# Routing weights placed by two fp16 products per token in place of three bf16 ones, in a two-layer mixer and expert kernel

## The reference, cut to what matters

```python
def one_block(xb):
    q = (xb @ w_q).reshape(tb, PEER_HEADS, 2, PEER_KEY_DIM)
    sc = jnp.einsum('thpk,hpnk->thpn', q, sub_keys).astype(jnp.float32)
    s1, i1 = lax.top_k(sc[:, :, 0], PEER_TOPK)
    s2, i2 = lax.top_k(sc[:, :, 1], PEER_TOPK)
    ...
    top_s, pos = lax.top_k(cand, PEER_TOPK)
    idx = jnp.take_along_axis(cidx, pos, axis=-1)
    gw = jax.nn.softmax(top_s, axis=-1).astype(xb.dtype)
    act = jax.nn.gelu(jnp.einsum('td,thkd->thk', xb, u[idx]), approximate=False)
    return jnp.einsum('thk,thkd->td', act * gw, v[idx])
```

## Time and profile before

| | |
|---|---|
| median of 3 runs | 1997.4 us (1996.92 to 1997.72) |
| profiled execution, its own time | 1997.13 us |
| its span on the core | 1995.2 us |
| granted TensorE clock, mean | 0.999 of full |
| TensorE busy | 1962.1 us, 98% |
| VectorE busy | 1267.2 us, 64% |
| ScalarE busy | 960.5 us, 48% |
| GpSimd busy | 1243.9 us, 62% |
| HBM traffic | 169 GB/s over the span |

### The profile page before, as it was taken

One profiled execution on the slowest core, in us unless ns is written; L12 is line 12 of the kernel. 1 busy time (PEld: TensorE's weight loads), 2 busy tenths in 40 slices (PEclk: granted clock), 3 DMA queues, 4 the chain that ended last, 5 costly groups with the idle time before them and its releaser, 6 DMA issues.

```text
span 1995.2 us, 40318 instructions
## 1 busy us (share of the span) xinstructions
PE 1962.1 (98%) x13590; PEld 1777.5 (89%) x13590; DVE 1267.2 (64%) x2812; ACT 960.5 (48%) x1521; POOL 1243.9 (62%) x624
## 2 busy tenths in 40 slices
PE   9999999999999999999999999999999999999998
PEld 9888999899999888888898889998999998888886
DVE  4753598479999444444456536974899984444444
ACT  5554445444434455455555544454444345454454
POOL 6436688876666555555474476888766665555553
PEclk9999999999999999999999999999999999999999
DMA  6524555544444555555545245555444445555553
GB/s 214 180 86 155 184 183 185 182 167 141 145 147 144 193 190 193 196 189 193 190 139 179 88 158 188 180 181 187 159 142 144 145 148 193 195 190 195 194 190 137
DMA packets 93244, 338.48 MB, mean 170 GB/s; under 512 B 10352, under 2 KB 10736, under 8 KB 93168
## 3 DMA queue, kind: packets, MB, share of 16 engines
q1 hardware_dynamic: 93168, 337.54, 50.5%
HBM read 336.45 MB, written 1.05 MB: 169 GB/s over the span
## 4 chain that ended last, share of the span: by engine, by line
PE 95%; DVE 3%; ACT 1%; DMA 1%; issue 0%; SPq 0%; DVEq 0%
PE PS L997 35%; PE PS L920 10%; PE PS L921 10%; PE PS L925 10%; PE PS L882 7%; PE PS L574 5%; PE PS L934 4%; PE PS L887 4%; PE PS L827 2%; PE PS L541 1%; PE PS L559 1%; PE PS L613 1%; PE PS L564 1%; PE PS L560 1%; PE PS L645 0%
## 5 line engine op out<-in xcount | busy, mean ns | idle before, releaser
L478 POOL TENSOR_TENSOR WL<-ring,WH 128x1024 fp32r<-128x1024 f32 x360 | 870.4, 2420 | 410.1 <-ACT WH L1238 223.8
L1238 ACT CAST WH<-ring 128x1024 fp32r<-128x1024 f32 x512 | 538.1, 1051 | 708.2 <-PE PS L997 327.0
L508 POOL TENSOR_TENSOR HX<-G,HX 128x256 fp32r<-128x256 f32 x256 | 371.3, 1450 | 325.5 <-ACT HX L1362 325.4
L1910 DVE TENSOR_TENSOR WL<-ring,WH 128x1024 fp32r<-128x1024 f32 x248 | 303.8, 1225 | 371.0 <-ACT WH L1238 371.0
L997 PE MATMUL PS<-WH,HX 128*128 128x512 f32 x2048 | 506.2, 389 | 3.0 <-issue 3.0
L997 PEld LDWEIGHTS PS<-WH,HX 128*128 128x128 f32 x2048 | 384.2, 188 | 83.1 <-issue 3.4
L920 PE MATMUL PS<-HX,WH 128*128 128x256 f32 x1664 | 418.3, 289 | 0.0
L921 PE MATMUL PS<-HX,WH 128*128 128x256 f32 x1664 | 407.7, 283 | 0.0
L921 PEld LDWEIGHTS PS<-HX,WH 128*128 128x128 f32 x1664 | 319.0, 192 | 0.0
L920 PEld LDWEIGHTS PS<-HX,WH 128*128 128x128 f32 x1664 | 318.4, 191 | 0.0
L1853 DVE SCALAR_TENSOR_TENSOR OH<-IOB,slotT,PS 128x384 bf16<-128x384 bf16 x512 | 307.8, 601 | 0.0
(11 more groups left out here) (247 smaller groups left out, 1907.0 us busy)
## 6 DMA issues: line engine op xcount, KB each, us to landing
ring<-stream SPq DMA_DIRECT2D x636, 512.0 KB, 3.3
X<-x_t SPq DMA_DIRECT2D x4, 256.0 KB, 3.9
out_t<-X SPq DMA_DIRECT2D x2, 512.0 KB, 2.7
CN<-consts SPq DMA_DIRECT2D x1, 851.0 KB, 9.4
WF<-last SPq DMA_DIRECT2D x1, 512.0 KB, 9.9
PR<-params SPq DMA_DIRECT2D x2, 239.0 KB, 4.2
CN<-consts SPq DMA_DIRECT2D x1, 64.0 KB, 4.2
```

The costliest lines, as they stand in the source:

```text
L478: nc.gpsimd.tensor_tensor(WL[:, b, :], ring[:, slot, :], WH[:, b, :].bitcast(F32), ALU.subtract).then_inc(done, 1)
L508: nc.gpsimd.tensor_tensor(GL[:, s, :], G[:, tile, :], GH[:, s, :].bitcast(F32), ALU.subtract).then_inc(L.gl_ready, 1)
L1238: nc.scalar.copy(WH[:, b, :], ring[:, slot, :]).then_inc(L.hi_ready, 1)
L1910: V.tensor_tensor(WL[:, s % 2, :], ring[:, (U0 + s) % SLOTS, :], WH[:, s % 2, :].bitcast(F32), ALU.subtract).then_inc(L.vlo_ready, 1)
```

## The change

The weights are multiplied by 2^15, so that they lie within fp16's range, and split into two fp16 parts instead of three bf16 ones. `O1` has 2 x 128 columns, and `place` issues two products for a token. The scale is taken back where the placed weights leave PSUM: in `weigh` the tensor_tensor becomes a scalar_tensor_tensor with 1/2^15, and in `keep` the copy becomes an activation with that scale. The preparation of the parts is three instructions in place of six. `O2`, the iota rows and the weight parts in SBUF are fp16 in place of bf16, of the same size per element.

```diff
-        OH = sb("OH", [P, 8, OW + 3 * P], BF16)
-        IOB = sb("IOB", [P, 3 * IW + P], BF16)
+        OH = sb("OH", [P, 8, OW + 2 * P], F16)
+        IOB = sb("IOB", [P, 3 * IW + P], F16)
...
                         for i in range(4):
                             o = bank[6 + g][:, i * P:(i + 1) * P]
-                            for a in range(3):
+                            for a in range(2):
                                 mm = nc.tensor.matmul(o, O2[:, 4 * g + i, 0:P], O1[:, 4 * g + i, a * P:(a + 1) * P],
-                                                      start=(a == 0), stop=(a == 2))
+                                                      start=(a == 0), stop=(a == 1))
...
-                        nc.scalar.copy(G[:, n:TILES, 4 * g:4 * g + 4], w[:, n:TILES, :]).then_inc(L.w_used, 1)
+                        nc.scalar.mul(G[:, n:TILES, 4 * g:4 * g + 4], w[:, n:TILES, :], 1 / W_SCALE).then_inc(L.w_used, 1)
...
-                    step(V.tensor_copy(WB[:, 0, :, :], w_whole))
-                    V.tensor_copy(w_part[0], WB[:, 0, :, :])
-                    step(V.tensor_tensor(w_part[2], w_whole, WB[:, 0, :, :], ALU.subtract))
-                    step(V.tensor_copy(WB[:, 1, :, :], w_part[2]))
-                    V.tensor_copy(w_part[1], WB[:, 1, :, :])
-                    V.tensor_tensor(w_part[2], w_part[2], WB[:, 1, :, :], ALU.subtract).then_inc(L.rt_free, 1)
+                    step(V.tensor_scalar(WB[:, :, :], w_whole, W_SCALE, None, ALU.mult))
+                    V.tensor_copy(w_part[0], WB[:, :, :])
+                    V.scalar_tensor_tensor(out=w_part[1], in0=w_whole, scalar=W_SCALE, in1=WB[:, :, :], op0=ALU.mult,
+                                           op1=ALU.subtract).then_inc(L.rt_free, 1)
...
-                            parts = PS[:, 2 + t // P, 0:3 * P].rearrange("p (a n) -> p a n", a=3)[:, :, t % P]
-                            ins = V.scalar_tensor_tensor(out=O1[:, slot, :].rearrange("p (a n) -> p a n", a=3),
-                                                         in0=bc(iota1, 1, 3), scalar=slotT[:, 0, t:t + 1],
+                            parts = PS[:, 2 + t // P, 0:2 * P].rearrange("p (a n) -> p a n", a=2)[:, :, t % P]
+                            ins = V.scalar_tensor_tensor(out=O1[:, slot, :].rearrange("p (a n) -> p a n", a=2),
+                                                         in0=bc(iota1, 1, 2), scalar=slotT[:, 0, t:t + 1],
                                                          in1=bc(parts, 2, P), op0=ALU.is_equal, op1=ALU.mult)
...
-                        V.tensor_tensor(acts, acts, w[:, 0:n, :], ALU.mult).then_inc(L.w_mul, 1)
+                        V.scalar_tensor_tensor(out=acts, in0=w[:, 0:n, :], scalar=1 / W_SCALE, in1=acts, op0=ALU.mult,
+                                               op1=ALU.mult).then_inc(L.w_mul, 1)
```

More of the change, by code:

```diff
@@ L24 @@
 F32R = mybir.dt.float32r
-BF16 = mybir.dt.bfloat16
+F16 = mybir.dt.float16
 U32 = mybir.dt.uint32
@@ L68 @@
 OW, IC, IW = 132, 43, 44
+W_SCALE = 2.0 ** 15
 TILES = EXPERTS // P
@@ L307, in program @@
         slotT = sb("slotT", [P, 2, SEQ])
-        WB = sb("WB", [P, 2, TT, P], BF16)
-        OH = sb("OH", [P, 8, OW + 3 * P], BF16)
-        IOB = sb("IOB", [P, 3 * IW + P], BF16)
+        WB = sb("WB", [P, TT, P], F16)
+        OH = sb("OH", [P, 8, OW + 2 * P], F16)
+        IOB = sb("IOB", [P, 3 * IW + P], F16)
         STG = sb("STG", [P, 2, 2, SEQ])
@@ L405, in program @@
         O2 = OH[:, :, 0:OW]
-        O1 = OH[:, :, OW:OW + 3 * P]
+        O1 = OH[:, :, OW:OW + 2 * P]
         iota3 = IOB[:, 0:3 * IW].rearrange("p (a b) -> p a b", a=3)
@@ L411, in program @@
         w_whole = PS[:, 2:4, 3 * P:4 * P]
-        w_part = [PS[:, 2:4, a * P:(a + 1) * P] for a in range(3)]
+        w_part = [PS[:, 2:4, a * P:(a + 1) * P] for a in range(2)]
         GH, GL = HH, HL
```

## The result

The changed kernel takes 1969.01 us, median of 4 runs (1967.62 to 1969.36), against 1997.56 us (1996.92 to 1999.32, 4 runs): a ratio of 0.9854, 95% interval 0.9842 to 0.9866. It is 28.6 us faster. The forecast was 1968.5 us, with a range of 1966 to 1972.

The account below looks back on a forecast made before the run. TensorE alone was taken to bound the kernel. Removing 512 placing products was worth -28.8 us, all else 0: 1997.13 us became 1968.3, the runs' median 0.3 higher, stated as 1968.5 us, range 1966 to 1972.

Parts of the forecast that it names:

- TensorE alone sets it: Placing stretch: groups follow at a constant 3.62 us though VectorE is full too, so TensorE alone sets the pace.
- The term of the sum: Placing on TensorE: four products fewer in each of 128 groups, 512 in all, worth 28.8 us (28.2 to 29.3).
- fp16 costs nothing: Placing products on TensorE: fp16 in place of bf16 changes their time by 0.
- rival A: Placing products: fp16 goes at the float32 price, 0.119 us each in place of 0.055; 2034 us, chance 4%.
- Rows shorter by 0.13 us: VectorE's `O1` one-hot row: 128 elements fewer take it from 0.52 to 0.39 us, 0.52 us less in a group.
- The weighing at +0.065 us: VectorE's weigh: scalar_tensor_tensor in place of tensor_tensor costs up to 0.065 us more in a group.
- The slack at the fullest: VectorE late in the stretch: 6.48 us of work against TensorE's 6.79 in two groups, 0.3 us of slack.
- the waits for line 935: Placing stretch: VectorE was to wait for TensorE's placing products everywhere, as a sign that the forecast is right.
- Rival B: VectorE becomes the bound late in the stretch if the `O1` row keeps its 0.52 us; 1981.5 us, chance 4%.
- Preparation, `keep`, weighing: Preparation about 1.2 us less VectorE work a layer, worth 0; `keep` about +0.02 us a group, hidden; weighing up to +0.065 us.
- Rival C: A hand-off between engines holds the period near 3.62 us: little or no gain, up to 1997 us; chance 2%.
- The other chain: ScalarE's cast, GpSimd's difference and the ring must follow a TensorE 6% quicker; 3.1 us of slack, so they keep up.

Follow-up runs that it names:

- experiment 1: Changed kernel with three products per token again (second part's product issued twice), the 256-column rows kept: 1996.83 us, ratio 0.9994.
- Experiment 4: Changed kernel with one product per token, rows of 256 columns still built on VectorE: 1939.07 us, ratio 0.9704.
- Experiment 3: Changed kernel with bfloat16 in place of float16 for the rows and parts: 1968.80 us, ratio 0.9850.
- experiment 5: Changed kernel with a scale of 1 and the old forms, tensor_tensor in weigh and a copy in keep: 1969.43 us, ratio 0.9850.
- experiment 2: Kernel before with two products per token in place of three, its 384-column rows, bf16 and preparation kept: 1979.96 us, ratio 0.9907.
- experiments 5 and 6: The former has its own line; the latter is the changed kernel with the preparation's first two instructions done four times over: 1969.67 us, ratio 0.9853.
- last experiment: Changed kernel with two groups placed together and one fp16 part per weight, so one product per token and 128-column rows: 1935.65 us, ratio 0.9689.

## Why the prediction was right

**The bound.** "TensorE alone sets it", read from a pace of 3.62 us that never changed although VectorE was full, held: with the old number of products and 3.35 us of 30 freed on VectorE the time did not move (experiment 1).

**The term of the sum.** It said 28.8 us, 0.0563 us for each of 512 products, between bounds of 28.2 and 29.3. The stretches gave 29.43: 0.0575 us each, 0.1 us above the upper bound. The small miss is in how a product of the middle was priced: by the two timelines the block went from 0.66 to 0.43 us, so each of the four removed took 0.057 to 0.058. Experiment 4 repeats the price from two products to one. The medians differ by 28.6 us and the profiled spans by 28.2, less than the stretches give, through the scatter outside them. So it is in part luck that the measured median lies within 0.5 us of the forecast: the term was 0.6 us too small, and the scatter went the other way.

**fp16 costs nothing.** The value taken was 0, with the float32 price as the other end. Experiment 3 settles it on both engines; rival A is out. Its price had been read too high as well: the 32 products of line 907 start at 227.54 us and the next product at 231.11 (rows below), which is 0.112 us each. The 0.119 of the prediction holds the tail of the last one. With 0.112 rival A would have stood at about 2027 us in place of 2034.

**VectorE.** Rows shorter by 0.13 us: measured 601 to 471 ns, right. The slope behind it was misread, without harm: the weighed tiles go from 256 to 496 elements, not to 512, so 671 - 411 ns belong to 240 elements, 1.08 ns each, which gives 0.14 us. The weighing at +0.065 us was an upper bound taken as a value, and was wrong by its size: 3 to 7 ns (median 546, against 543 in experiment 5 and 539 before). The slack at the fullest, forecast as 6.79 - 6.48 = 0.3 us in two groups, turned out somewhat larger, and the waits for line 935 that were forecast everywhere stand late in the stretch in every second group only. The changed kernel's timeline shows VectorE idle 0.39 to 0.42 us once in two groups late in the stretch:

```profile
608.72 0.65 DVE L1866 SCALAR_TENSOR_TENSOR G<-PS,G 128x472 f32<-128x472 f32 x1 [0.42 <-PE PS L935]
...
612.14 0.65 DVE L1866 SCALAR_TENSOR_TENSOR G<-PS,G 128x480 f32<-128x480 f32 x1
...
615.50 0.66 DVE L1866 SCALAR_TENSOR_TENSOR G<-PS,G 128x480 f32<-128x480 f32 x1 [0.39 <-PE PS L935]
```

Rival B named the right neighbour. Its condition, rows that stay at 0.52 us, is nearly what experiment 2 builds, without the dearer weighing that rival B counted in: the prediction gave 1981.5 us for it, measured 1979.96.

**What was hidden.** Preparation, `keep`, weighing: experiments 5 and 6 moved each back or made it longer. Their runs, 1967.5 to 1970.8 us, overlap those of the changed kernel, and their stretches are as long as its own.

**The other chain.** Rival C had 3.1 us of slack against it; the chain of cast, difference and ring holds no one up even at 3.13 us a tile (last experiment). At which pace it would begin to was not tried.

## What to carry to other kernels

When two engines are full, look at whether the pace of the work changes where the second one gets heavier: if it does not, the first one alone is the bound, and its removed instructions are worth their start-to-start time. But then work out the new pace against the second engine's load part by part: here the same edit of TensorE is worth 29 us with the shorter rows and 18 us without. Narrow products between wide ones also cost something for each block, apart from their number (0.06 us here), so put them together as far as the neighbours' deadlines allow.

## What the runs showed of the hardware

- A block of 128-column products among 256-column ones costs more than its products: the second wide product behind it starts 0.20 us after the first, where the others follow at 0.12. With half as many blocks two tiles took about 6.72 us in place of 6.78, and the kernel 3.5 us less. It is no matter of 16 bits: in the kernel before the same 0.20 us (231.11 to 231.31) stands behind the 128-column float32 products of line 907. Both kinds of block differ from the wide products in width and in type, and no run here tells which of the two counts.

```profile
227.54 3.81 PE L907 MATMUL PS<-ring,G 128*128 128x128 f32 x32 [0.45 <-ACT G L1280]
231.11 0.36 PE L920 MATMUL PS<-HX,WH 128*128 128x256 f32 x1
231.31 0.28 PE L921 MATMUL PS<-HX,WH 128*128 128x256 f32 x1
```

- fp16 and bf16 cost the same here: 218 ns for a product of 128 columns in either type, 471 against 472 ns for the row instruction, and the stretch is as long to 0.01 us (experiment 3).
- On VectorE a scalar_tensor_tensor with a constant as its scalar takes what a tensor_tensor of the same elements takes (415 against 411 ns at 256 elements). The two that take their scalar from SBUF are 56 to 65 ns longer at 256 elements (471 ns for line 1852, 476 for line 1454). That the scalar's place is the reason is only argued; the types of the operands differ too.
- An activation with a scale is 13 to 17 ns longer than a copy of the same elements in `keep` (shortest, median and longest 182, 280 and 381 ns, against 169, 266 and 364 for the copy of experiment 5). Against the kernel before (160, 272 and 368 ns) it is 8 to 22.
